# Gate modulation of a transformer layer on TensorE: sixteen single groups put into eight pairs

## What is computed

```python
cond = jax.nn.silu(c)
mod = cond @ mod_w[i] + mod_b[i]
sh_m, sc_m, gt_m, sh_f, sc_f, gt_f = jnp.split(mod[:, None, :], 6, axis=-1)
h = rms_norm(x, norm_g[i, 0]) * (1.0 + sc_m) + sh_m
y = swa_sink_attention(h, swa_w_qkv[j], swa_w_o[j], swa_sinks[j], cos, sin)
x = x + gt_m * rms_norm(y, norm_g[i, 1])
h = rms_norm(x, norm_g[i, 2]) * (1.0 + sc_f) + sh_f
x = x + gt_f * rms_norm(swiglu(h, ffn_w_in[i], ffn_w_out[i]), norm_g[i, 3])
```

## Time and profile before

| | us |
|---|---|
| median of 3 runs | 1140.44 (1139.5 to 1140.71) |
| the profiled execution | 1141.52 |
| its span, first to last instruction | 1139.7 |
| TensorE busy in the span | 1066.1 (94%) |
| VectorE busy | 697.2 (61%) |
| ScalarE busy | 467.5 (41%) |
| GpSimd busy | 63.0 (6%) |

### The profile page before, as it was taken

One profiled execution on the slowest core, in us unless ns is written; L12 is line 12 of the kernel. 1 busy time (PEld: TensorE's weight loads), 2 busy tenths in 40 slices (PEclk: granted clock), 3 DMA queues, 4 the chain that ended last, 5 costly groups with the idle time before them and its releaser, 6 DMA issues.

```text
span 1139.7 us, 13583 instructions
## 1 busy us (share of the span) xinstructions
PE 1066.1 (94%) x4968; PEld 844.9 (74%) x4968; DVE 697.2 (61%) x866; ACT 467.5 (41%) x554; POOL 63.0 (6%) x59
## 2 busy tenths in 40 slices
PE   5788899898897799999999999999999999999995
PEld 2555766576685588888888888888888888888884
DVE  2686777978897836676675444445443555445544
ACT  4322454443553643443333333333334433444333
POOL 0000012301210100000000000000001000000002
PEclk9899999998999999999999999999999999999998
DMA  9999999997797327787776555555555455555532
GB/s 363 416 416 416 416 362 388 404 353 263 286 356 295 130 92 259 268 314 264 295 304 212 187 184 199 189 188 194 184 185 185 167 202 184 186 196 205 185 147 74
DMA packets 50599, 288.23 MB, mean 253 GB/s; under 512 B 6401, under 2 KB 6401, under 8 KB 23937
## 3 DMA queue, kind: packets, MB, share of 16 engines
q1 hardware_dynamic: 47090, 268.47, 63.4%
q0 software_dynamic: 2304, 16.78, 3.6%
q10 hardware_dynamic: 1168, 2.49, 0.6%
HBM read 285.36 MB, written 2.10 MB: 252 GB/s over the span
## 4 chain that ended last, share of the span: by engine, by line
PE 77%; DVE 8%; DMA 8%; ACT 3%; issue 2%; POOL 1%; SPq 0%; DVEq 0%; ACTq 0%; POOLq 0%
PE ps L1271 24%; PE ps L1272 24%; PE ps L1273 24%; DMA mraw<-in_mod_w 4%; DMA graw<-in_mod_h 4%; PE ps L1294 3%; DVE wlo L718 3%; DVE mraw L729 2%; ACT whi L399 2%; PE ps L1328 1%; PE ps L1428 1%; PE ps L1304 1%; DVE nT L769 0%; PE ps L1317 0%; DVE wlo_in L718 0%
## 5 line engine op out<-in xcount | busy, mean ns | idle before, releaser
L718 DVE TENSOR_TENSOR wlo<-raw,whi 128x1024 fp32r<-128x1024 f32 x336 | 400.5, 1233 | 308.7 <-ACT whi L399 308.7
L1271 PE MATMUL ps<-whi,hThi 128*128 128x512 f32 x1232 | 488.5, 396 | 20.4 <-DVE wlo L718 18.0
L399 ACT ACTIVATE whi<-raw 128x2048 fp32r<-128x2048 f32 x168 | 321.5, 1916 | 413.3 <-PE ps L1273 390.8
L1273 PE MATMUL ps<-whi,hTlo 128*128 128x512 f32 x1232 | 483.0, 392 | 0.0
L1272 PE MATMUL ps<-wlo,hThi 128*128 128x512 f32 x1232 | 482.9, 392 | 0.0
L1271 PEld LDWEIGHTS ps<-whi,hThi 128*128 128x128 f32 x1232 | 233.4, 189 | 85.9 <-issue 35.1
L1273 PEld LDWEIGHTS ps<-whi,hTlo 128*128 128x128 f32 x1232 | 233.1, 189 | 49.6
L1272 PEld LDWEIGHTS ps<-wlo,hThi 128*128 128x128 f32 x1232 | 233.7, 190 | 47.3
L729 DVE CUSTOM_DVE_ANT_0 mraw<-mraw,cb,mbias 128x1024 f32<-128x1024 f32 x64 | 88.0, 1389 | 45.0 <-DMA mraw<-in_mod_w 45.0
L729 DVE CUSTOM_DVE_ANT_0 mraw<-mraw,cb,modT 128x1024 f32<-128x1024 f32 x64 | 83.6, 1318 | 20.6 <-DMA mraw<-in_mod_w 20.4
L1271 PE MATMUL ps<-whi,oThi 128*128 128x512 f32 x112 | 46.6, 416 | 9.2 <-DVE wlo L718 9.2
(11 more groups left out here) (150 smaller groups left out, 535.1 us busy)
## 6 DMA issues: line engine op xcount, KB each, us to landing
raw<-in_w_in SPq DMA_DIRECT2D x88, 1024.0 KB, 4.8
mraw<-in_mod_w SPq DMA_DIRECT2D x128, 512.0 KB, 7.6
raw<-in_w_out SPq DMA_DIRECT2D x44, 1024.0 KB, 4.8
raw<-in_w_qkv SPq DMA_DIRECT2D x24, 1024.0 KB, 11.4
graw<-in_mod_h SPq DMA_DIRECT2D x16, 1024.0 KB, 14.7
graw<-in_mod_h POOLq DMA_DIRECT2D x16, 1024.0 KB, 8.7
raw<-in_w_o SPq DMA_DIRECT2D x16, 1024.0 KB, 7.2
x<-in_x ACTq DMA_DIRECT2D x2, 1024.0 KB, 8.9
```

Of the source, the lines that this page charges most:

```text
L399: A(split_of(q, s)[0], raw[:, s], ACT.Copy).then_inc(hi_done, 1)
L718: V.tensor_tensor(low[:, k], raw[:, s, k], high[:, k].bitcast(F32), ALU.subtract).then_inc(done, 1)
L1271: mm(dst, hi, high[:, n], start=start, stop=False)
L1273: return mm(dst, lo, high[:, n], start=False, stop=stop)
```

## The change

TensorE's order between blocks 12 and 23 is written anew; nothing else changes. The sixteen gate groups, of which each stood alone between two other pieces of work, now stand in pairs, an even one and the odd one behind it, in eight places. Blocks 12, 15, 16, 19 and 20, which were cut into halves around a group, are taken whole. `columns(5)` moves from behind group 24 to ahead of it. GpSimd, VectorE, ScalarE and SyncE have the same instructions in the same order as before, GpSimd's wait for the buffers included.

```diff
-            q_block(12, (0,))
+            q_block(12)
             gate_sums(16)
-            q_block(12, (1,))
             gate_sums(17)
             q_block(13, (0,))
             k_turn()
             q_block(13, (1,))
             q_turn(0)
             gate_sums(18)
+            gate_sums(19)
             q_block(14, (0,))
             scores(0)
             q_block(14, (1,))
-            gate_sums(19)
-            q_block(15, (0,))
+            q_block(15)
             gate_sums(20)
-            q_block(15, (1,))
             gate_sums(21)
             columns(4)

-            q_block(16, (0,))
+            q_block(16)
             gate_sums(22)
-            q_block(16, (1,))
             gate_sums(23)
             q_block(17, (0,))
             p_turn(0)
             q_block(17, (1,))
             q_turn(1)
             outputs(0)
+            columns(5)
             gate_sums(24)
-            columns(5)
+            gate_sums(25)
             q_block(18, (0,))
             scores(1)
             q_block(18, (1,))
-            gate_sums(25)
-            q_block(19, (0,))
+            q_block(19)
             gate_sums(26)
-            q_block(19, (1,))
             gate_sums(27)

-            q_block(20, (0,))
+            q_block(20)
             gate_sums(28)
-            q_block(20, (1,))
             gate_sums(29)
             columns(6)
...
             outputs(1)
             gate_sums(30)
+            gate_sums(31)
             q_block(22, (0,))
             scores(2)
             q_block(22, (1,))
-            gate_sums(31)
             q_block(23)
```

## The result

| | us |
|---|---|
| before, median of 6 runs | 1140.58 |
| changed, median of 6 runs | 1150.89 (1144.73 to 1156.03) |
| changed / before | 1.0092, 95% interval 1.0067 to 1.0118 |
| profiled execution of the changed kernel, its span | 1144.73, 1142.9 |

The change makes the kernel slower by 10 us, 0.92%. The forecast was 1147.7 with a range of 1142 to 1152.5. Two further series of the same kernel gave medians of 1151.8 (ratio 1.0099) and 1153.8 (1.0108), the last above the range.

What follows compares the result with a forecast made beforehand. TensorE was taken to lead from 142 to 250 us, with DMA 98% busy beside it. Terms -2.3 -5.6 +13.9 +1.3 = +7.3 us on the median 1140.44 gave 1147.7 us, range 1142 to 1152.5.

Steps and rivals of the forecast that it cites:

- part 1: Gate groups before 238.88 us: seven pairs each save 0.33 us of interruption on TensorE, -2.3 us.
- part 2: TensorE, 142 to 250 us: the five old waits for gate weights all go, -5.6 us.
- part 3: Pairs 18/19, 22/23, 24/25, 28/29: both loads queue together, so TensorE waits anew for the second, +13.9 us.
- part 4: Inside 18/19: a 4.0 us wait lowers TensorE's granted clock for ten matmuls or less, +1.3 us.
- The chain behind it: From ScalarE's high part of block 23 on: TensorE's 7 us delay shifts everything behind it; nothing gives it back.
- A: Gate loads keep up as SyncE's queue falls silent: new waits 4.4 us, no clock loss, 1136.9 us; chance 0.08.
- B: SyncE's queue stays busy everywhere: new waits 17.5 us, clock falls twice for 2.6 us, 1152.6 us; chance 0.17.
- C: Behind 238.88 us the column loads set the chain, so TensorE's delay makes no odds: 1140.4 us; chance 0.06.

Runs made afterwards that it cites:

- noload_pair: Changed order (pairs) with gate loads 18 to 31 left out, against the kernel before: 1133.12 us, ratio 0.9939.
- noload_single: Kernel before (single groups) with gate loads 18 to 31 left out: 1134.19 us, ratio 0.9947 to before.
- warm: Changed kernel with 42 filler matmuls where TensorE would stand idle for gate loads: 1147.35 us, ratio 1.0064 to before.
- again: Changed kernel run a second time, unaltered: 1151.8 us, ratio 1.0099 to before; its trace is of the execution of 1146.33 us.
- after: First profile of the changed kernel, unaltered, of the execution of 1144.73 us; median of that series 1150.89 us.
- again2: Changed kernel run a third time, unaltered: 1153.8 us, ratio 1.0108 to before; its trace is of the execution of 1147.2 us.
- early_pairs: Kernel before with only groups 16 to 23 in four pairs (blocks 12, 15, 16 whole): 1147.18 us, ratio 1.0038.
- late_pairs: Kernel before with only groups 24 to 29 in three pairs (blocks 19, 20 whole, columns(5) moved): 1146.41 us, ratio 1.0033.
- deep_pair: Changed kernel with more gate-load buffers and loads started as buffers come free: 1146.77 us, ratio 1.0046 to before.

## Why the forecast came near, step by step

The direction, the place and the chain were right: waits for the second of two gate loads that queue up together, on a chain that passes all of it on to ScalarE's high part of block 23 (243.99; some 246 was forecast). The sizes by term, in us; "measured" is by medians of whole runs except for the waits:

| term | forecast | measured |
|---|---|---|
| part 1, fewer interruptions | -2.3 | -1.1 (noload_pair against noload_single), not told from 0 |
| part 2, the old waits | -5.6 | -6.0 (noload_single against before, the loads' share of the DMA with it) |
| part 3, new waits | +13.9 | 11.0, 10.3, 10.7 idle in three traces; 14.2 with all they bring (warm against noload_pair) |
| part 4, the clock | +1.3 | +4.5 (again against warm, by medians), 3.7 at 28/29 in one trace |
| sum | +7.3 | +11.6 (again), 10.3 in the first series, 12.9 in the third |

The 11.6 is no check on the terms: with 14.2 for part 3, each kernel is set against the next, and their differences must add up to it. The check is the trace: 7.1 us from waits, clock and pairs, where 7.4 were lost.

**Part 1.** Right in sign at most. The 0.33 us per pair is what the trace shows around one; whole runs show half of it, and an interval that holds zero.

**Part 2.** Right within what the run can tell, since leaving the loads out takes more away than the waits.

**Part 3.** By place, forecast and then the traces of the changed kernel (after, again, again2): inside 18/19 4.6, and 1.8, 2.8, 2.6; around 22/23 2.3, and 3.3, 3.1, 3.1; 24/25 0.5, and none; 28/29 6.5, and 5.9, 4.5, 5.0. The first was the miss. I had both loads share the DMA with SyncE's queue, but SyncE issued its next block only at 148.47, 1.1 us behind the first of the two, which was issued at 147.35 and landed in 5.7 us; the second took 9.9 and not 12.5. The earlier trace rows did show SyncE's block starting only at 149.49, three us behind the 146.50 of load 18 there; I read it as "in flight" all the same. That the late block made the landings short fits these times, and no run tests it. At 28/29 the landing was as worked out in one trace, 12.7, and shorter in again and again2, 10.8 and 11.4. The idle time was thus sized 3 us too high. The 14.2 between warm and noload_pair is a wider thing: it holds also what the loads take from the others' share of the DMA (0.94 against 0.76), and fillers beyond the idle time. I can't split it further.

**The chain behind it.** I had said that nothing gives the delay back. The chain of the changed kernel, and then that of before, each at ScalarE's last step ahead of the long second half:

```profile
401.32 1.16 ACT y L646
```

```profile
396.81 1.16 ACT y L646
```

Of the 5.1 us at 243.99, 4.5 arrive there, and 3.2 at the end. With the 1.9 us by which this execution came earlier into the stretch, the loss is 7.0 us at the high part of block 23, 6.4 at 400 us and 5.1 at the end. So the passing on was right as far as 400 us, but for 0.6; 1.3 us come back in the 740 us behind, where both kernels have the same instructions in the same order, and the cause is open.

**Part 4** is the step that failed. I took one dip of the clock, inside 18/19, and left one at 28/29 for the range; the criterion was that a wait must be longer than the 3.14 us of the earlier trace rows. Instead the clock fell at 28/29 in every trace of the changed kernel, for some 10 us, and at 18/19 and 22/23 only in again2, after waits of 2.60 and 2.34 us, less than that criterion. That cost 3.7 us at 28/29 alone in the first trace, and 4.5 by the medians of again and warm, not 1.3. (The 1.3 is also less than its own words: ten matmuls at 0.43 instead of 0.227 us would be 2.0.) That the forecast of 1147.7 came within 3.2 us of the 1150.89 is in part luck: against the traces, the idle time was put 3 us too high and the clock 2 to 3 us too low, so that the lost time in the stretch, 7.3 forecast and 7.0 measured, agrees better than its terms do. The whole runs lie 10 to 13 us above before; why most of them are longer than the executions traced stays open.

**The rivals.** A (the loads keep up, new waits of 4.4 us) fell: the second loads of the pairs took 9.9 to 12.7 us in the first trace. By the fit in the Trainium skill's page "DMA: Bandwidth & Descriptors", section "Anatomy of one DMA — SWDGE (gpsimd) path", such a load would take an estimated 4.4 us; no 1 MB gate load in any trace here did, the least being 5.1 us (early_pairs). By the Trainium skill's page "DMA: Bandwidth & Descriptors", section "Queues, rings and completion order", each DMA engine takes turns between the queues, packet by packet; that second loads took 9.9 us and more with SyncE's loads in flight fits with it. B, the full price, had the waits wrong (17.5) but the clock nearer the truth (2.6). C, absorbed, fell: the high part of block 23 came 5.1 us late and the span with it, 3.2 us in that execution, and the medians by 10. My later belief that two thirds of the loss sat at 28/29 fell with early_pairs (0.38%) and late_pairs (0.33%).

**What stays open.** The three traces of the changed kernel are of executions of 1144.7 to 1147.2 us; what those at 1152 add isn't in any trace. Some 4.5 us of the loss, by the medians, goes with fillers alone, so it is clock and not data, and the mean clock of the long executions is lower; that it is more dips of the kind seen in again2 is argued, not shown. What decides whether a wait brings the clock down is open too: 2.77 us did not in again, 2.39 did in early_pairs and 1.34 in deep_pair. Nor did I try pairs with the two loads started apart on their own queue.

## What to carry to other kernels

Work that is grouped to save switches takes from a pair of buffers the lead that their loads had: compare the work between two groups with the landing of the second of two queued loads beside what the other queues move at that moment, not with the median of single ones. On TensorE count such a wait more than once: in this kernel gaps of 1.3 to 3.6 us could bring the clock down, which cost 3.7 us at one place on top of 5.9 us of idle time, and matmuls that nobody reads, put into the gap, kept the clock up. And when DMA is at 98%, more buffers buy little: 2.8 us here, where leaving the loads out bought 6.0.

## What the runs showed of the hardware that I had not expected

Two waits of only 2.08 and 2.16 us, four us apart and with slow or small work between them (late_pairs), were followed by a granted clock of 0.53 over 11 us, the 1.2 GHz level nearly throughout. The length of a wait alone didn't tell what the clock would do. It fell after a single wait of 2.39 us (early_pairs) and even of 1.34 us behind small matmuls (deep_pair, 0.83 over 10 us), and stayed at 1.00 after waits of up to 1.8 us (before) and after one of 2.77 us (again). Waits of 0.7 to 1.0 us and then some 2.35 us, around 22/23, left it alone in two executions of the changed kernel (after, again) and brought it down in another (again2). Fillers in the gaps kept it at 1.00, though TensorE was the busiest engine; by the medians the kernels were 4.5 us and, each against its own kernel before, 1.8 us faster, neither size well fixed. The same order of instructions showed one dip in one execution and three in another, while the changed kernel's executions spread over 11 us (1144.73 to 1156.03).
